# Inverting the 32x32 diagonal blocks of a delta rule on GpSimd, two chunks at a time, instead of on TensorE

## What is computed

```python
lower = jnp.where(strict, jnp.einsum('bhncd,bhnsd->bhncs', k_beta, k) * decay, 0.0)
system = lower + jnp.eye(C, dtype=lower.dtype)
sol = lax.linalg.triangular_solve(system, rhs, left_side=True, lower=True)
...
v_new = u_c - jnp.einsum('bhcd,bhde->bhce', w_c, state)
o_c = jnp.einsum('bhcd,bhde->bhce', q_c, state) + jnp.einsum('bhcs,bhse->bhce', a_c, v_new)
state = state * jnp.exp(gl_c)[..., None, None] + jnp.einsum('bhcd,bhce->bhde', kd_c, v_new)
```

## Time and profile before

| | us |
|---|---|
| median of 3 runs | 2550.47 (2544.6 to 2553.95) |
| the profiled execution | 2535.64 |
| its span, first to last instruction | 2533.9 |
| PE busy in the span | 2312.9 (91%) |
| DVE, ACT, POOL busy | 1082.2, 906.8, 390.6 |

### The profile page before, as it was taken

The page is one execution under the profiler, slowest core; times in us unless marked ns, Lnnn a source line. Parts: engine busy times, 40 slices in busy tenths (PEclk is TensorE's granted clock), DMA queues, the critical chain, the costliest instruction groups (busy, mean ns, idle before and its releaser), DMA issues. The chain is left out here.

```text
span 2533.9 us, 47637 instructions
## 1 busy us (share of the span) xinstructions
PE 2312.9 (91%) x17494; PEld 1329.8 (52%) x17495; DVE 1082.2 (43%) x2488; ACT 906.8 (36%) x2283; POOL 390.6 (15%) x630
## 2 busy tenths in 40 slices
PE   6999999999779999999999997799966999999990
PEld 2545545455356666666666665355534444444440
DVE  2434333343346666666666565133344222222223
ACT  2263462633635555555555544011110010101112
POOL 1000000000111001000000000233221222222224
PEclk9999999999979999999999999899987999999995
DMA  9212121111263213211222103733311879999787
GB/s 335 73 67 76 51 82 44 55 63 36 89 163 106 76 54 95 86 58 63 71 72 80 41 27 155 270 113 129 125 67 50 245 215 309 270 324 301 217 237 290
DMA packets 187895, 334.49 MB, mean 132 GB/s; under 512 B 19723, under 2 KB 119718, under 8 KB 184502
## 3 DMA queue, kind: packets, MB, share of 16 engines
q1 hardware_dynamic: 173878, 281.51, 32.8%
q0 software_dynamic: 13824, 50.34, 8.2%
HBM read 242.36 MB, written 89.44 MB: 131 GB/s over the span
## 5 line engine op out<-in xcount | busy, mean ns | idle before, releaser
L708 PE MATMUL pV<-mod_rows_then_work,w_in_sb 128*128 128x512 f32 x768 | 340.7, 597 | 4.4 <-DMA w_in_sb<-in_w_in_dram 4.4
L2079 PE MATMUL hidden_ps<-w,keys_values_then_all 128*128 x752 | 331.5, 594 | 1.2 <-SPq L1951 1.2
L1147 ACT ACTIVATE probs<-scores,neg_max 128x512 f32<-128x512 f32 (+3 forms) x320 | 199.6, 624 | 332.0 <-DVE neg_max L1276 218.5
L1430 PE MATMUL scores<-keys_values_then_all,queries 96*128 96x512 f32 (+3 forms) x640 | 303.5, 557 | 7.6 <-DMA keys_values_then_all<-kp_d 7.6
L2079 PEld LDWEIGHTS hidden_ps<-w,keys_values_then_all 128*128 128x128 f32 x752 | 143.2, 191 | 181.7 <-issue 181.7
L708 PEld LDWEIGHTS pV<-mod_rows_then_work,w_in_sb 128*128 128x128 f32 x768 | 144.7, 191 | 177.5 <-issue 176.8
L1728 PE MATMUL out_ps<-keys_values_then_all 128*128 128x512 f32 x512 | 226.2, 600 | 2.5 <-ACT keys_values_then_all L1593 2.5
L1435 PE MATMUL bank<-ident,probs 128*128 128x128 f32 x1088 | 183.4, 284 | 1.5 <-ACT probs L1147 1.2
L2009 ACT ACTIVATE keys_values_then_all<-hidden_ps 128x256 f32<-128x256 f32 x47 | 18.0, 384 | 455.7 <-PE hidden_ps L2079 455.7
L1276 DVE TENSOR_REDUCE neg_max<-scores 128x1 f32<-128x512 f32 x192 | 132.2, 688 | 111.5 <-PE scores L1430 110.4
L1447 PE MATMUL outT_ps<-probs_T,keys_values_then_all 128*64 128x128 f32 x2176 | 156.3, 282 | 22.2 <-issue 18.5
(11 more groups left out here) (367 smaller groups left out, 3337.9 us busy)
## 6 DMA issues: line engine op xcount, KB each, us to landing
w<-in_w_dram SPq DMA_DIRECT2D x64, 1024.0 KB, 10.0
w_sb<-in_w_dram SPq DMA_DIRECT2D x32, 1024.0 KB, 14.2
w_mod_rows<-in_w_mod_dram SPq DMA_DIRECT2D x16, 1024.0 KB, 4.8
kqv<-qkv_d SPq DMA_DIRECT2D x16, 768.0 KB, 4.3
mod_rows_then_work<-in_w_mod_dram SPq DMA_DIRECT2D x4, 2048.0 KB, 15.0
x_in<-in_x_dram SPq DMA_DIRECT2D x16, 512.0 KB, 3.5
qkv_d<-l_out SPq DMA_DIRECT2D x32, 256.0 KB, 2.3
keys_values_then_all<-y_d SPq DMA_DIRECT2D x16, 512.0 KB, 5.0
```

What stands on the lines that cost most here:

```text
L708: last = pe.matmul(pV[n % 2][:], win[:, k, QKV0 + c * P:QKV0 + (c + 1) * P], hT[:, s % 2, k, :], start=(k == 0), stop=(k == ND - 1))
L1147: act.activation(prob[:, e, 0:w].rearrange("p t k -> p (t k)"), pS[e][:, 0:w * P], ACT.Exp, scale=-1.0, bias=nmin[:, i % 2, h, b:b + 1], a ...
L1430: pe.matmul(pS[e][:, 0:w * P], qT[:, i % 2, slot(h)], kT[:, 4 * b:4 * b + w, slot(h), :], start=True, stop=True).then_inc(s_ready, 1)
L2079: last = pe.matmul(pH[par][:], xT[par][:, k], m.w13[:, ds(slot, 1), k].rearrange("p s n -> p (s n)"), start=(k == 0), stop=(k == ND - 1))
```

## The change

The 32x32 diagonal blocks are no longer inverted on PE. NLV goes from 6 to 2: only the joins to 64 and 128 stay as steps Y and WU. In their place POOL runs a forward substitution. A group is two chunks: 2 chunks x 4 blocks x 4 heads give 32 matrices, one on each of the partitions 96 to 127, in a corner of the key tile that is not used otherwise. For each column j POOL multiplies (outer product into `outer`) and subtracts, on (31-j)(j+1) elements each, 31 columns, and every instruction waits for the one ahead of it; two fills come first, and a transposing copy of 1024 elements last. The work is cut into 16 pieces, steps I, eight in each of the two turns of a group.

Data go through DRAM. Each chunk's A and the query product are stored (`a_d`, `qk_d`, step KA), the blocks are loaded to the corner (LB, four DMAs), the inverses of a group are stored (IS), and step L loads for each chunk seven sets of blocks, A again, and the query product again. K runs four chunks ahead of the recurrence in place of one, from a tile of its own (`kk`). The gate tile has two buffers instead of three. AS stands behind all pairs of the following tile instead of one pair behind A. POOL's masks in `projection` and the steps U0, KB, W0 and D are gone.

```diff
-LVB, BL = 5, 32
+BL = 32
+AHEAD, BATCH = 4, 2
+PIECES = 16
...
+def spread(steps, between):
+
+    if not between:
+        return steps
+    cut = [k * len(steps) // len(between) for k in range(len(between) + 1)]
+    return [x for k, piece in enumerate(between) for x in [piece] + steps[cut[k]:cut[k + 1]]]
...
+        if i and (hp, b) == (AH // 2 - 1, TILE[i] // 4):
+            atoms.append((0.0, [("AS", i - 1, 0)]))
         if (hp, b) == (AH // 2 - 1, TILE[i] // 4):
             atoms.append((0.0, [("B", i, 0)]))
-        if i and o == (AH // 2 if TILE[i] >= 4 else AH // 2 - 1):
-            atoms.append((0.0, [("AS", i - 1, 0)]))
...
-    for c in range(-2, NT):
-        n, d = c + 1, c + 2
-        prep, rec = 0 <= n < NT, c >= 0
-        steps += [(1.0, ("K", n)), (0.5, ("KA", n)), (0.5, ("U0", n)), (0.5, ("KB", n))] * prep
-        steps += [(0.45, ("VT", c)), (0.45, ("KD", c)), (1.0, ("KS", c)), (0.7, ("QS", c)), (0.85, ("TR", c))] * rec
-        steps += [(0.7, ("W0", n)), (0.8, ("Y", n, 1))] * prep
-        steps += [(0.85, ("DS", c))] * rec
-        steps += [(0.9, ("WU", n, 1)), (0.8, ("Y", n, 2))] * prep
...
+    for c in range(-AHEAD, NT):
+        n, a, d = c + 1, c + AHEAD, c + AHEAD + 1
+        first, prep, rec = a < NT, 0 <= n < NT, c >= 0
+        g, half = (c + 3) // BATCH, (c + 3) % BATCH
+        pieces = [(0.8 if c < 0 else 0.0, ("I", g, k)) for k in range(half * PIECES // 2, (half + 1) * PIECES // 2)]
+        pieces *= 0 <= g < NT // BATCH
+        lead = [(1.0, ("K", a)), (0.5, ("KA", a))] * first
+        lead += [(0.45, ("VT", c)), (0.45, ("KD", c)), (1.0, ("KS", c)), (0.7, ("QS", c))] * rec
+        lead += [(0.0, ("LB", a))] * (first and not half)
+        lead += [(0.85, ("TR", c))] * rec
+        body = [(0.8, ("Y", n, 1))] * prep
+        body += [(0.85, ("DS", c))] * rec
+        body += [(0.9, ("WU", n, 1))] * prep
+        tail = [(0.85, ("AV", c))] * rec
+        tail += [(0.8, ("Y", n, 2))] * prep
+        tail += [(0.0, ("O1", c))] * rec
+        late = [(0.9, ("M", k)) for k in MOD_AT.get(c, ())[:-1]]
+        late += [(0.5, ("WU", n, 2))] * prep
+        late += [(0.0, ("G", d))] * (d < NT)
+        late += [(0.9, ("M", k)) for k in MOD_AT.get(c, ())[-1:]]
+        late += [(0.0, ("O2", c))] * rec
+        mid = [(0.0, ("IS", g))] * (half and len(pieces) > 0) + [(0.0, ("LB", a))] * (half and first)
+        if half:
+            turn = spread(lead + body, pieces) + tail + mid + late
+        else:
+            turn = lead + spread(body + tail + late, pieces)
+        turn += [(0.0, ("L", c + 2))] * (0 <= c + 2 < NT)
+        steps += turn
...
-    NLV = 6
+    NLV = 2
...
+            def load_kk(c):
+                sp.dma_start(kk[:], m.qkv_d[c:c + 1, :, 0:2 * GH].rearrange("t p c i -> p (t c) i")).then_inc(kk_loaded, 16)
+
+            def store_products(c):
+                wait(lt_ready, c + 1)
+                sp.dma_start(m.a_d[c * P:(c + 1) * P, :], lt_new[:].rearrange("p h i -> p (h i)")).then_inc(lt_stored, 16)
+                wait(at_ready, c + 1)
+                sp.dma_start(m.qk_d[c * P:(c + 1) * P, :], at_new[:].rearrange("p h i -> p (h i)")).then_inc(at_stored, 16)
+
+            def load_blocks(c):
+                wait(lt_stored, 16 * (c + 1))
+                wait(inv_ready, c // BATCH)
+                for q in range(4):
+                    at_row = (c % BATCH * 4 + q) * GH
+                    sp.dma_start(Ab[at_row:at_row + GH], m.a_d[c * P + BL * q:c * P + BL * (q + 1), :].rearrange(
+                        "j (h r i) -> h r j i", h=GH, r=4)[:, q]).then_inc(block_loaded, 16)
+
+            def load_inverses(c):
...
+                wait(inv_stored, 16 * (c // BATCH + 1))
+                wait(xw_ready, NLV * c)
+                wait(tr_ready, c - 1)
+                if c == 0:
+                    sp.wait_ge(zero_made, 3)
+                for q in range(4):
+                    rows = m.inv_d[(c * 4 + q) * GH:(c * 4 + q + 1) * GH, :].rearrange("h (k i j) -> i h k j", k=2, i=BL)
+                    sp.dma_start(U[c % 2][quarter[q], :, quarter[q]], rows[:, :, 1]).then_inc(blocks_back, 16)
+                    if q < 3:
+                        dst = Wh[quarter[q], :, quarter[q]] if q < 2 else Wb[quarter[q]]
+                        sp.dma_start(dst, rows[:, :, 0]).then_inc(blocks_back, 16)
+                sp.dma_start(lt[:].rearrange("p h i -> p (h i)"), m.a_d[c * P:(c + 1) * P, :]).then_inc(lt_loaded, 16)
+                wait(av_ready, c - 1)
+                wait(at_stored, 16 * (c + 1))
+                sp.dma_start(at[c % 2][:].rearrange("p h i -> p (h i)"), m.qk_d[c * P:(c + 1) * P, :]).then_inc(at_loaded[c % 2], 16)
...
+                elif kind == "IS":
+                    wait(inv_ready, n + 1)
+                    sp.dma_start(m.inv_d[n * (P - QK):(n + 1) * (P - QK), :], both_T).then_inc(inv_stored, 16)
+                elif kind == "L":
+                    load_inverses(n)
...
+            def then(ins):
+                done[0] += 1
+                ins.then_inc(inv_step, 1)
+                pool.wait_ge(inv_step, done[0])
+
+            def invert(g, piece):
+                n = P - QK
+                wait(em_ready, made["G"])
+                wait(o_pow, 2 * made["O1"])
+                wait(a_pow, 2 * made["A"])
+                if piece == 0:
+                    pool.wait_ge(cpad_made, 2)
+                    pool.wait_ge(state_zero, 1)
+                    pool.wait_ge(bias_zero, 1)
+                    pool.wait_ge(zero_made, 3)
+                    wait(inv_stored, 16 * g)
+                    then(pool.memset(both_T[:, 0:BL * BL], 0.0))
+                    then(pool.memset(both_T[:, 0:BL * BL:BL + 1], 1.0))
+                    pool.wait_ge(block_loaded, 16 * 4 * BATCH * (g + 1))
+                for j in range(piece * BL // PIECES, (piece + 1) * BL // PIECES):
+                    below, upto = BL - 1 - j, j + 1
+                    if below:
+                        prod = outer[:, 0:below * upto].rearrange("p (i c) -> p i c", i=below)
+                        then(pool.tensor_tensor(prod, Ab[:, j, j + 1:].unsqueeze(2).to_broadcast([n, below, upto]),
+                                                Tb[:, j:j + 1, 0:upto].to_broadcast([n, below, upto]), ALU.mult))
+                        then(pool.tensor_tensor(Tb[:, j + 1:, 0:upto], Tb[:, j + 1:, 0:upto], prod, ALU.subtract))
+                if piece == PIECES - 1:
+                    pool.tensor_copy(Ub, Tb.rearrange("p i j -> p j i")).then_inc(inv_ready, 1)
+                    wait(inv_ready, g + 1)
...
-                elif kind == "KB":
-                    wait(ltb_ready, n + 1)
-                    wait(xw_ready, NLV * (n - 1) + LVB - 1)
-                    pool.tensor_tensor(xt[:, 1:], ltb[:].unsqueeze(1).to_broadcast([P, LVB - 1, GH, BL]),
-                                       mask_b[:, 1:].unsqueeze(2).to_broadcast([P, LVB - 1, GH, BL]), ALU.mult).then_inc(xt_ready, 1)
...
-                elif kind == "W0":
-                    wait(w0_ready, n + 1)
-                    act.copy(WU[:, :, 0], bank[at_bank[step][0]][:, :, 0:BL]).then_inc(w0_copied, 1)
...
-                elif kind == "D":
-                    wait(u_updated, (LVB - 1) * (n + 1))
-                    wait(xw_ready, NLV * n)
-                    wait(tr_ready, n - 1)
-                    act.wait_ge(zero_made, 3)
-                    for q in quarter[0:2]:
-                        act.copy(Wh[q, :, q], WU[q, :, 0])
-                    for q in quarter[2:4]:
-                        last = act.copy(U[n % 2][q, :, q], WU[q, :, 1])
-                    last.then_inc(diag_ready, 1)
...
-                elif kind == "WU" and step[2] < LVB:
-                    wait(u_ready, NLV * n + step[2])
-                    dve.tensor_tensor(WU[:], WU[:], bank[at_bank[step][0]][:, :, 0:2 * BL].rearrange("p h (two c) -> p h two c", two=2),
-                                      ALU.subtract).then_inc(u_updated, 1)
...
-                elif kind == "W0":
-                    wait(u0_ready, n + 1)
-                    for h in range(GH):
-                        for q in quarter:
-                            last = pe.matmul(bank[b0][q, h, 0:BL], WU[q, h, 1], ident_b[q], start=True, stop=True)
-                    last.then_inc(w0_ready, 1)
...
-                        if lv < LVB:
-                            for q in quarter:
-                                last = pe.matmul(bank[b0][q, h, 0:BL], xt[q, lv, h], WU[q, h, 0], start=True, stop=True)
...
-                        if lv < LVB:
-                            for q in quarter:
-                                pe.matmul(bank[b0][q, h, 0:BL], WU[q, h, 1], Yb[q, h], start=True, stop=True)
-                            for q in quarter:
-                                last = pe.matmul(bank[b0][q, h, BL:2 * BL], Yb[q, h], WU[q, h, 1], start=True, stop=True)
```

176 lines of the change are left out of this document (74 added, 102 removed).

## The result

The changed kernel takes 2473.84 us (median of 4 runs, 2469.71 to 2480.03), the kernel before 2547.53 us (4 runs, 2543.08 to 2553.95). The ratio is 0.9711 with a 95% interval from 0.968 to 0.9742: 74 us faster. The profiled execution took 2474.45 us against 2535.64 us, 61.2 us less; the sum in the prediction had said 58.7 less. The forecast was 2492 us, the range 2458 to 2550 us, so the time is within the range and 18 us under the forecast. Of these, 15 us come from the reference point: the forecast added the 15 us by which the profiled run of before lay under its median, and the profiled run of after lies at its own. The sum itself missed by 2.5 us.

What follows compares the result with a forecast made beforehand. `mix` was taken as bound by PE's issue of matmuls. Terms -74.7 - 12 + 13 + 8 + 3 + 4 = -58.7 us, from a median of 2550.5, gave 2492 us; range 2458 to 2550.

Steps and rivals of the forecast that it cites:

- The small matmuls, -74.7 us: PE in `mix`: each of 16 chunks loses W0, four Y and four WU, 4.67 us, together 74.7 us.
- The waits in the chain, -12 us: PE's waits inside the inversion chain and at the joins mostly go: 12 us saved, between 4 and 14.
- the +3 us for V: PE waits at V behind more bare transposition and score pairs: 3 us lost, between -8 and 15.
- The late `em`, +13 us: In K, DVE waits for POOL's `em` behind four columns, and PE loses time: 13 us, from 0 to 35.
- The norm in the first tiles, +8 us: Start of `mix`: POOL reaches norm A behind its pieces, holding up in-order ACT: 8 us, from 0 to 15.
- The last turns, +4 us: Turns without G and M: POOL's norm and O2 come close together, 1 to 2 us in three turns, 4 us.
- DMA, 0 us: The new stores and loads, and SP's wait in IS, are all covered: 0 us.
- 6 us ahead of SyncE in IS: At the store of the inverses, POOL has finished some 6 us earlier, so nothing behind it is held.
- Rival 1: POOL stays ahead everywhere, so the 13, 8 and 4 us fall away: 2467 us; chance 0.13.
- Rival 2: POOL slower by half, 64 us a group: 2593 us; decides from 56 us a group; chance 0.16 with rival 4.
- rival 4: PE doesn't shorten; V and T wait for DVE and ACT, 80 us: 2560 us; chance 0.16 with Rival 2.
- Rivals 3: Small DMAs slow or SP late, Y waits for L, 32 us: 2524 us; 0.23, shared with dearer POOL.

Runs made afterwards that it cites:

- a_g_early: The changed kernel with the decay mask step G put ahead of POOL's pieces in turns that start a group: 2445.19 us, ratio 0.9608.
- g_small_apart: `a_g_early` plus 160 extra PE steps of 16 matmuls of 32x32, results unused: 2510.93 us.
- b_no_levels: The kernel before with levels 1 to 4 of the 32x32 inversion left out and nothing in their place: 2478.64 us, ratio 0.9762.
- a_loads_late: The changed kernel with five of SyncE's first loads issued behind the first stores of the products or first scores: 2469.72 us, ratio 0.9705.
- a_as_back: The changed kernel with the attention-norm scaling AS back where the kernel before has it: 2470.36 us, ratio 0.9704.
- a_mul_x3: The changed kernel with every multiply on POOL issued three times: 2601.55 us, ratio 1.0244.

## Why the prediction came out as it did

**The small matmuls, -74.7 us.** Mis-sized. PE's busy time fell by 103.0 us where `em` is not late (724.2 in `a_g_early`, 827.2 in before), 28 more than priced. The step that failed is the distance from a step's start to its successor's, which leaves out the lengthening of the step ahead. 144 small steps at the 0.13 more that `g_small_apart` shows (0.52 against 0.39) are 19 us of the 28. The rest is the clock, which I left out knowingly. Both kernels start `mix` partly at the lower level, before for longer; the first 80 us, before and then `a_g_early`, and a stretch of before:

```profile
680.00:760.00 80.00, 50.69 (x684) 0.70 0.60 161
```

```profile
680.00:760.00 80.00, 43.54 (x262) 0.81 0.66 183
```

```profile
739.70:753.30 13.60, 13.13 (x55) 0.50 0.47 135
```

Added over all stretches of `mix` at 0.50, PE is busy 42.0 us in before, 47.6 in after and 16.4 in `a_g_early`. Four transpositions take 1.08 us at the lower level and 0.60 at the upper, so 25.6 us less at the lower level should save about 11 us (an estimate), and 74.7 + 19 + 11 is 105. The same estimate gives 14 us for the 31.2 us between after and `a_g_early`, where 14.1 were measured. How much of the difference in the first 80 us is due to the edit and how much changes from one execution to the next, one trace of each kernel doesn't show.

**The waits in the chain, -12 us.** They went, all of them. But `b_no_levels` shows that idle time didn't fall (66.5 to 71.6 us): V took them over. As a saving of the whole this term and the +3 us for V belong together, and they are about +5, not -9.

**The late `em`, +13 us.** The mechanism, the place and the size of one wait were right (2.4 to 3.0 us, about every second turn; 13.5 us in five waits). By `a_g_early` this term and the next cost 29 us together, where I had 21. What failed is that I priced the idle time and not the clock behind it, 14.1 us.

**The norm in the first tiles, +8 us.** It is there: ACT waits 6.3 us for `attn_rstd` in two pieces, and PE idles 6.13 us at 766.73. 4.2 of them go when the mask stands first, so the late `em` was the larger part of this too.

**The last turns, +4 us.** Not what happened: from 1210 us to the end of `mix` no wait of PE is above 1.7 us. The handoff cost 7.1 us, through the y store behind the loads of the output stage. The prediction had costed the moved scaling only for the first tiles; of a moved step its store's place on SyncE counts too.

**DMA, 0 us.** Wrong at two places. The first store took 11 us to be seen. DVE, which writes the product of the second chunk to the same buffer, waited 8.66 us for it, and PE idled 7.11 us; `a_loads_late` shows that this is not simply to be had back. And at 819.83 PE idled 7.72 us because ACT waited for a y store:

```profile
818.58 0.63 ACT L1233 ACTIVATE attn_y<-attn_out 128x512 f32<-128x512 f32 x1 [8.09 <-DMA y_d<-attn_y]
```

SyncE issued that store at 805.48, behind 25 other DMAs from 789.88 on, LB, IS and L among them, and it landed 13 us later. Without POOL's products this wait is as long (9.17 us), and with the scaling in its early place (`a_as_back`) it is gone: it belongs to the late place and to the queue.

I had also said that POOL would be 6 us ahead of SyncE in IS. SyncE waited there for POOL in five groups, none of them the first:

```profile
SPq L1052 <- POOL keys_values_then_all L1131: 45.1, 5, 11.4
```

The reading was wrong, but it cost PE nothing that shows: in `a_g_early` SyncE waits there as long (44.5 us), and `mix` is as short as without POOL's products.

**The rivals.** Rival 1 (POOL ahead everywhere) is what `a_g_early` makes true: 2445 us, under the 2467 of that rival since PE's term was too small. Rival 2 is real, `a_mul_x3` is slower than before; it decides at about 63 us a group, not 56, and so further from the 40 us measured. The 2560 us of rival 4 were a slip: 2492 + 80 is 2572. Rivals 3 and 4 fail: PE never waits at Y for a DMA in the changed kernel, and its matmul time fell by more than priced. V's waits passed the 30 us that I had named as a sign against the forecast (36.0 us), and the forecast held all the same only because PE's own term was short by about as much.

## What to carry to other kernels

Before work is put on a half-idle in-order engine, list what small products of others that engine makes and put these ahead of the new pieces: here one 1.27 us product in the wrong place cost as much as 40% of the whole gain. Price a wait of PE in otherwise full work twice, once as idle time and once as a stretch at the lower clock behind it; here the two were the same size in sum, though not each wait had such a stretch. Price a step of small matmuls by adding steps to a kernel and reading PE's busy time, not from the distance of two starts; and look for the value of a moved store or load in the waits within the next 30 us before counting it as saved.
